# GpSimd in place of VectorE for the low halves of the weight strips, in a two-block transformer kernel on one core

## What is computed

```python
x = x + jnp.concatenate([mix, mem_o], axis=-1) @ w_out[l]
x = x + conv_ffn(rmsnorm(x, g_ffn[l]), w_up[l], w_dw_f[l], b_dw_f[l], w_down[l])
```

## Time and profile before

| | us |
|---|---|
| median of 3 runs (3259.78, 3284.76, 3285.53) | 3284.76 |
| profiled execution, whole | 3262.2 |
| its span, first to last instruction | 3260.4 |
| TensorE busy | 2917.2 |
| VectorE busy | 1568.1 |
| ScalarE busy | 1090.7 |
| GpSimd busy | 2.7 |

### The profile page before, as it was taken

How to read it: one execution, slowest core, us unless ns; L and a number is a source line. 1 busy time by engine, 2 the same in 40 slices (tenths; PEclk the granted TensorE clock), 3 DMA queues, 4 the chain that set the end, 5 groups by cost and what they waited for, 6 DMA issues and landing times.

```text
span 3260.4 us, 32364 instructions
## 1 busy us (share of the span) xinstructions
PE 2917.2 (89%) x12615; PEld 2219.1 (68%) x12615; DVE 1568.1 (48%) x2487; ACT 1090.7 (33%) x1655; POOL 2.7 (0%) x17
## 2 busy tenths in 40 slices
PE   5885699999999999999897888899988997799997
PEld 4650277877865677778686656678767865687785
DVE  3349656546433446464624464533346356533235
ACT  3220233323333334242434632422236433332222
POOL 0000000000000000000000000000000000000000
PEclk8979899999985689999897889999999979899998
DMA  4229423332220013333221001223322200132231
GB/s 126 78 98 404 156 78 100 94 91 77 85 91 1 1 39 91 90 92 88 81 78 55 1 1 39 77 80 102 89 92 65 91 1 1 52 91 82 86 97 46
DMA packets 316965, 259.55 MB, mean 80 GB/s; under 512 B 15093, under 2 KB 306702, under 8 KB 316814
## 3 DMA queue, kind: packets, MB, share of 16 engines
q1 hardware_dynamic: 316442, 257.34, 25.3%
q10 hardware_dynamic: 372, 0.14, 0.0%
HBM read 255.36 MB, written 2.10 MB: 79 GB/s over the span
## 4 chain that ended last, share of the span: by engine, by line
PE 81%; DVE 9%; ACT 3%; issue 2%; DVEq 2%; PEld 1%; PEldq 1%; ACTq 1%; SPq 0%; DMA 0%
PE ps L348 49%; PE ps L364 6%; PE ps L360 5%; PE ps L368 5%; PE ps L1367 5%; PE ps L1390 4%; DVE y L1246 3%; PE ps L1380 2%; DVE wL L318 2%; ACT wH L304 1%; PE ps L1370 1%; PE ps L828 1%; PE ps L1484 1%; DVEq L1248 1%; PEldq L1604 1%
## 5 line engine op out<-in xcount | busy, mean ns | idle before, releaser
L318 DVE TENSOR_TENSOR wL<-raw,wH 128x2048 fp32r<-128x2048 f32 (+1 forms) x186 | 416.2, 2238 | 1051.0 <-ACT wH L304 1050.2
L304 ACT ACTIVATE wH<-raw 128x2048 fp32r<-128x2048 f32 (+1 forms) x186 | 348.1, 1872 | 1186.2 <-PE ps L348 843.2
L348 PE MATMUL ps<-hH,wH 128*128 128x512 f32 (+1 forms) x1656 | 420.6, 396 | 0.0
L348 PE MATMUL ps<-hH,wL 128*128 128x512 f32 (+1 forms) x1656 | 419.8, 396 | 0.0
L348 PE MATMUL ps<-hL,wH 128*128 128x512 f32 (+1 forms) x1656 | 419.8, 396 | 0.0
L348 PEld LDWEIGHTS ps<-hH,wH 128*128 128x128 f32 x1656 | 311.1, 189 | 75.5 <-issue 1.0
L348 PEld LDWEIGHTS ps<-hL,wH 128*128 128x128 f32 x1656 | 311.3, 189 | 75.0
L348 PEld LDWEIGHTS ps<-hH,wL 128*128 128x128 f32 x1656 | 311.3, 189 | 75.0
L360 PE MATMUL ps<-gH,wH 128*128 128x512 f32 x480 | 157.3, 415 | 18.5 <-ACT wH L304 18.5
L1367 PE MATMUL ps<-kS,qS 64*128 64x256 f32 (+3 forms) x288 | 155.7, 635 | 17.9 <-ACTq L1412 17.9
L364 PE MATMUL ps<-gH,wL 128*128 128x512 f32 x480 | 155.0, 409 | 10.7 <-DVE wL L318 10.7
(11 more groups left out here) (305 smaller groups left out, 3697.3 us busy)
## 6 DMA issues: line engine op xcount, KB each, us to landing
raw<-w_up SPq DMA_DIRECT2D x132, 512.0 KB, 5.2
mod_ring<-w_mod SPq DMA_DIRECT2D x64, 768.0 KB, 6.4
raw<-w_down SPq DMA_DIRECT2D x32, 1024.0 KB, 5.1
raw<-w_gate SPq DMA_DIRECT2D x44, 512.0 KB, 4.0
raw<-w_down SPq DMA_DIRECT2D x16, 768.0 KB, 4.4
raw<-w_in_odd SPq DMA_DIRECT2D x12, 1024.0 KB, 5.2
raw<-w_in_even SPq DMA_DIRECT2D x9, 1024.0 KB, 5.1
raw<-w_out SPq DMA_DIRECT2D x8, 1024.0 KB, 5.2
```

The source lines that it names most:

```text
L304: last = act.activation(wH[:, st.slot, 0:st.size], raw[:, st.slot, 0:st.size], ACT.Copy)
L318: last = dve.tensor_tensor(wL[:, st.slot, 0:st.size], raw[:, st.slot, 0:st.size], wH[:, st.slot, 0:st.size].bitcast(F32), ALU.subtract)
L348: last = pe.matmul(dst, left, right, start=(t == 0 and k == 0), stop=(t == 2 and k == self.kt - 1))
```

## The change

The low halves are formed by GpSimd, in the order of the strips, in one loop after its constants; the signal that a low half is there comes from GpSimd. VectorE's calls are gone from all places. Where a strip has a gain, GpSimd first multiplies the raw strip by the gain in place, in eight pieces, drains, and then subtracts over the whole strip; VectorE had done both in one instruction for each piece.

```diff
-        weights_high, weights_low = Signal("weights_high", "act"), Signal("weights_low", "dve")
+        weights_high, weights_low = Signal("weights_high", "act"), Signal("weights_low", "pool")
...
-        def split_low(dve, n):
+        def split_low(pool, n):
...
-            dve.wait_ge(weights_high.sem, START + n + 1)
+            pool.wait_ge(weights_high.sem, START + n + 1)
             if st.gain is None:
-                last = dve.tensor_tensor(wL[:, st.slot, 0:st.size], raw[:, st.slot, 0:st.size], wH[:, st.slot, 0:st.size].bitcast(F32),
+                last = pool.tensor_tensor(wL[:, st.slot, 0:st.size], raw[:, st.slot, 0:st.size], wH[:, st.slot, 0:st.size].bitcast(F32),
                                          ALU.subtract)
             else:
                 for k in range(st.kt):
                     part = slice(k * st.width, k * st.width + st.width)
-                    last = dve.scalar_tensor_tensor(wL[:, st.slot, part], raw[:, st.slot, part], col(st.gain[0], st.gain[1] + k),
-                                                    wH[:, st.slot, part].bitcast(F32), ALU.mult, ALU.subtract)
+                    pool.tensor_scalar(raw[:, st.slot, part], raw[:, st.slot, part], col(st.gain[0], st.gain[1] + k), None, ALU.mult)
+                pool.drain()
+                last = pool.tensor_tensor(wL[:, st.slot, 0:st.size], raw[:, st.slot, 0:st.size], wH[:, st.slot, 0:st.size].bitcast(F32),
+                                          ALU.subtract)
             last.then_inc(weights_low.sem, 1)
...
             def vector(self, dve):
                 for s, st in self.numbered():
-                    split_low(dve, st.n + 2)
                     self.run.open_vector(dve, st)
                     self.vector_take(dve, s, st)
...
                         if self.run.prepare is not None and s == 0:
-                            split_low(dve, st.n + 2)
                             self.run.open_vector(dve, st)
...
-                        if not (self.run.prepare is not None and s == 0):
-                            split_low(dve, st.n + 2)
...
                     gate_in, value = st.tiles
-                    split_low(dve, st.n + 2)
                     dve.wait_ge(tile_done.sem, value.done)
...
             pool.drain().then_inc(constants_in, 1)
+            for n in range(len(Strip.made)):
+                split_low(pool, n)
...
             start_signals(dve, "dve")
-            split_low(dve, 0)
-            split_low(dve, 1)
```

## The result

The change makes the kernel slower: 3367.02 us median (3362.03 to 3386.45, 4 runs) against 3285.15 us (3259.78 to 3306.23), a ratio of 1.0264 with a 95% interval of 1.018 to 1.0347. Whether it is slower by more than 2% is open. The profiled execution took 3368.79 us, its span is 3367.0 us, so 106.6 us more than the profile of before. That pair of profiles overstates the change: the one of before was among its faster runs.

What follows compares the result with a forecast made beforehand. TensorE, 89% busy and 81% of the chain, was taken as the bound. 21 + 6 + 3.5 + 14 - 12.9 - 8 - 1 = +22.6 us gave 3285 or 3307 us by baseline; forecast 3296, between them, range 3255 to 3340.

Steps and rivals of the forecast that it cites:

- A GpSimd subtraction: Low half of a 2048-element strip: 4.4 us on GpSimd against VectorE's 2.3; 3.3 against 1.77 for 1536 elements.
- The pair with a gain: Products with a gain, at 832 us: 2.5 us net at the pair, 1 us after the narrow strip, together 3.5.
- the 15 us of room: Mid-run, TensorE asks for a low half one strip and two tile passes later, leaving 15 us for its chain.
- Pairs and clock: Runs beginning with two strips: 21 us at ten eight-tile pairs, 6 at four six-tile pairs, 14 for clock falls.
- VectorE within the runs: Convolution's up part: 2.3 us of VectorE's work per strip goes, worth nothing; if held by GpSimd, still in time.
- The ends of stages: Five barriers: without the low half VectorE takes at once, 3.5 us at 956 and 2.1 to 2.5 elsewhere, -12.9 us.
- The norms: Four norms: VectorE's last taking, sums and squares come sooner; -17.9 or -3.4 us, taken as -8.
- the holding rival: One engine keeps the other out of SBUF for a whole instruction: +35 us, 3297 us, chance 0.26.
- The first barrier: Its 5.1 us wait for VectorE shrinks, with GpSimd's passes beside VectorE's tables: -1 us, between 0 and -4.4.
- SyncE: Strip loads wait for the low half two strips back: slot free 2.1 us later, hidden; perhaps 1 us late in memory stage.
- The stretched pass: Rival: both engines continue slowly, a pass beside VectorE's work takes some 6 us; net +61, 3323 us, chance 0.19.
- The relief: Rival: a 3.25 us pass, no extra clock falls or collisions, stage ends give 35.2 us; net -22, 3240 us, chance 0.18.

Runs made afterwards that it cites:

- the mixed kernels: The change with a flag per strip choosing VectorE or GpSimd for its low half; successively returning gain strips, pairs, first up parts to VectorE gave 1.0132, 1.0086, 1.0059 of before.
- the constant factor: Against the change, GpSimd multiplies strips with a gain by the constant 1.0 instead of the column of gains; one run, 3335.44 us.

## Why the prediction was wrong

It gave 3296 us in a range of 3255 to 3340 and most of its chance to no measurable change. By its own steps, and with the differences between the mixed kernels outside attention (38.1 + 36.2 + 15.0 + 2.3 = 91.6 us):

- *A GpSimd subtraction, 4.4 us:* right, 4.66 on average (3.61 for 1536 elements, 3.3 assumed), 4.50 at the shortest. The rate of a stream read from the memset rows carried over to within a tenth; whether both inputs and the output take turns, as the sum had it, no run shows.
- *The pair with a gain, 2.5 us, and 1 us behind it:* the step that failed. The multiplications were given 0.25 to 0.45 us each by the same rates; they are 0.9, so 7.4 us a strip with the drain instead of 2.8. Seen as one more wait that is 4.6 us. It became 38 us because the 15 us of room were taken to hold at every strip with a gain but the pair's and the one behind the narrow strip. With 3.3 + 7.2 us of latency that hid almost everything; with 3.3 + 12 it does not. The pair wants two strips at once and gets them one after the other (4.82 + 11.59 us of wait), the strip behind it has 8.7 us of room, two others 13.3 and 9.3 (16.2 us in five waits in the run), and half the clock follows each of the long ones. The strip behind the pair was missed even by the prediction's own numbers: 3.3 + 7.2 against 8.7 is 1.8 us that no term held. GpSimd's period of 11.9 us against TensorE's 11.25 matters little beside this, as the constant factor showed. The bound from rows rested on memset and affine_select, neither of which multiplies, and its upper end was taken for a wall.
- *Pairs and clock, 21 + 6 + 14 = 41 us:* about right in sum. The wait grew by 2.3 us (1.07 to 3.36) at most of the eight-tile pairs and by 1.7 to 1.8 us at the others; the clock fell at all fourteen, as expected. Alone they cost 47.1 us, put back they save 36.2. Less the waits (30.7 and 24.0 us) that leaves 16.4 and 12.2 us for the clock, near the 14 of the sum, though in the change itself it may be more: over 12 us from each restart PEclk sums to 10.9 of 14 instead of 13.1, which would be 26 us of full clock. One row of each kind, after: stretch, length, PE busy (x), PEclk, DMA share, GB/s (compare):

```profile
687.30:699.30 12.00, 11.93 (x42) 0.80 0.27 87
...
805.90:817.90 12.00, 11.89 (x40) 0.76 0.22 66
```

- *VectorE within the runs, "worth nothing" and still in time if held:* wrong at one kind of place. In a steady run the second and third up parts are indeed 90.0 and 67.5 us to the tenth. But the first up part begins with the root mean square, so VectorE starts a strip and more late; at 10.77 us a cycle (508.71 less 497.94, two rows of gL) against 11.25 it hardly catches up, and ScalarE, waiting behind it, brings the next pair's high half 4.1 us late. TensorE's rows at that boundary, before 1.69 and 1.07:

```profile
540.42 1.19 PE L362 MATMUL ps<-gH,wH 128*128 128x512 f32 x2 [5.80 <-ACT wH L304]
545.32 1.22 PE L366 MATMUL ps<-gH,wL 128*128 128x512 f32 x2 [2.86 <-POOL wL L318]
```

  Moving those strips back gives 15.0 us.
- *The ends of stages, -12.9 us:* right where a barrier follows. At the one of the earlier trace rows the chain after is

```profile
1008.44 1.91 ACT wH L304
...
1010.44 3.83 PE ps L1481 x7
```

  2.0 us instead of 5.6; at 182, 1821 and 2675 us it is 3.8, 2.3 and 4.0 instead of 6.2, 4.6 and 6.4. The one after the memory keys lost 1.8 us instead (6.42 before, 8.26 now), because VectorE's sinT was held by the pass. Together that is -8.9 us, and the 2.4 us at 182 do not come out in the time of the piece.
- *The norms, -8 us:* close to nothing. From TensorE's last product to its first of the next stage: 16.6, 18.3, 19.3 and 18.3 us after, 15.8, 19.1, 19.0 and 19.2 before, -0.6 in all. That is less than the lower of the two ends, -3.4; the holding rival foresaw the +0.8 at the first.
- *The first barrier, -1:* -4.8 us (the first product's statistics at 40.8 instead of 45.6 us), beyond the better of its two ends.
- *SyncE:* as said, about 1 us late in the memory stage.

Of the rivals, whole-instruction holding was the true one in its mechanism, and its 35 us was too little mainly because it carried the same 3.5 us for the gain strips: with 38 in their place it would have been 70, of the 91.6 measured. The stretched pass did not occur (4.66 us on average, 5.16 at the longest). The relief did not decide anywhere.

## What to carry to other kernels

Work that is moved to a slower engine has to be checked against the room at every kind of place where something waits for it, the rare ones too: not the 15 us of the usual strip, but the 8.7 us right behind a pair, the 9.3 us behind a narrow strip, and the pair, where two are wanted at once. Eleven of 197 strips made 42% of the loss, because a chain of 15.3 us met such rooms. A rate that matches the consumer's is not enough: with it, four fifths of that loss stayed. And an engine that holds up the one it relieves gives little back: VectorE lost 451 us of work and was 31 us less busy.

## What the runs showed of the hardware

- A GpSimd tensor_scalar of 128 x 256 float32 took about 0.9 us with a column as the factor and 844 ns on average with a constant, far above a memset's 0.25 us of the same size. It is not a cheap instruction beside a tensor_tensor of 2048 elements at 4.5 us: eight of them cover the same data in 7.24.
- VectorE's 128 x 512 instructions with two SBUF inputs, one copy and one tensor_scalar from SBUF to SBUF, waited for the whole GpSimd instruction in progress (up to 4.9 us for gL, 4.2 for the other two); those with a PSUM input, 0.69 us, and the reciprocal, 3.35 us, did not. Cutting GpSimd's pass into eighths let VectorE in (gL 2452 to 858 ns), at 1.9 us more for the pass.
- The same attention stage comes out at 231 or 248 us, and another between 267 and 302 us, in kernels that differ only in who forms the weights' low halves, with different granted clock (0.85 and 0.72; between 0.82 and 0.72). Between two profiles of one and the same kernel it made 19.5 of 20.3 us. That it makes all of the 60 us between that kernel's runs (3246 to 3306) is not shown.
